# Rotary half-swaps and key doublings issued from ScalarE's queue instead of SyncE's, in a two-layer NSA/FoX decoder trunk

## The reference

```python
proj = x @ w_in
q, kc, vc, ks, vs, kw, vw, gl = jnp.split(proj, cuts, axis=-1)   # 16 query heads, 4 groups of keys and values
def apply_rope(x, cos, sin):
    x1, x2 = jnp.split(x, 2, axis=-1)
    return x * cos + jnp.concatenate([-x2, x1], axis=-1) * sin
q_rot = apply_rope(q, cos, sin)
k_slc = apply_rope(kv_heads(ks), cos, sin)
k_win = apply_rope(kv_heads(kw), cos, sin)
out = g0 * attend(q, k_cmp, v_cmp) + g1 * attend(q_rot, k_slc, v_slc) + g2 * attend(q_rot, k_win, v_win)
```

## Time and profile before

| | |
|---|---|
| median of 3 runs | 1443.62 us (1443.61 to 1446.38) |
| the profiled execution | 1443.62 us, span 1441.8 us |
| TensorE busy | 1366.0 us (95%) |
| VectorE, ScalarE, GpSimd busy | 691.6, 671.3, 624.6 us |
| DMAs issued by SyncE | 126.63 MB, 30.1% of 16 DMA engines' span |

### The profile page before, as it was taken

One profiled execution on the slowest core, in us unless ns is written; L12 is line 12 of the kernel. 1 busy time (PEld: TensorE's weight loads), 2 busy tenths in 40 slices (PEclk: granted clock), 3 DMA queues, 4 the chain that ended last, 5 costly groups with the idle time before them and its releaser, 6 DMA issues.

```text
span 1441.8 us, 20004 instructions
## 1 busy us (share of the span) xinstructions
PE 1366.0 (95%) x7050; PEld 1122.2 (78%) x7050; DVE 691.6 (48%) x1312; ACT 671.3 (47%) x1249; POOL 624.6 (43%) x402
## 2 busy tenths in 40 slices
PE   8979999977999999999999999998899999999997
PEld 5857777766788888888888787877788888888886
DVE  3346767767174344341008477788184443442006
ACT  4346767666234444443112576777334444443110
POOL 2356767663335444444434222221334444444441
PEclk9999999999999999999999999999999999999999
DMA  9432221210523332333232322121423333324221
GB/s 281 98 74 52 45 52 47 55 40 1 176 59 102 102 101 88 102 101 132 88 96 67 95 76 60 45 80 55 160 74 88 102 90 99 102 88 145 88 74 58
DMA packets 170237, 127.59 MB, mean 88 GB/s; under 512 B 24032, under 2 KB 155860, under 8 KB 170164
## 3 DMA queue, kind: packets, MB, share of 16 engines
q1 hardware_dynamic: 170164, 126.63, 30.1%
HBM read 116.98 MB, written 4.39 MB: 84 GB/s over the span
## 4 chain that ended last, share of the span: by engine, by line
PE 75%; DVE 14%; issue 3%; ACT 3%; POOL 2%; DMA 1%; SPq 1%; DVEq 0%; POOLq 0%; ACTq 0%
PE ps L924 14%; PE ps L926 14%; PE ps L925 14%; PE ps L1166 7%; PE ps L1165 7%; PE ps L1168 7%; PE ps L1086 2%; PE ps L1100 2%; DVE ptl L1439 2%; DVE xt L1579 2%; DVE negmax L1422 1%; DVE xt L1569 1%; DVE stats L1573 1%; DVE prob L1435 1%; PE ps L1053 1%
## 5 line engine op out<-in xcount | busy, mean ns | idle before, releaser
L463 POOL TENSOR_TENSOR wl<-raw,wh 128x1024 fp32r<-128x1024 f32 x180 | 437.1, 2432 | 675.5 <-ACT wh L582 675.3
L924 PE MATMUL ps<-xh,wh 128*128 128x512 f32 x968 | 392.0, 405 | 0.2 <-POOL wl L463 0.2
L926 PE MATMUL ps<-xh,wl 128*128 128x512 f32 x968 | 378.8, 391 | 0.0
L925 PE MATMUL ps<-xl,wh 128*128 128x512 f32 x968 | 377.8, 390 | 0.0
L582 ACT ACTIVATE wh<-raw 128x1024 fp32r<-128x1024 f32 x192 | 201.6, 1052 | 211.1 <-PE ps L1168 200.9
L926 PEld LDWEIGHTS ps<-xh,wl 128*128 128x128 f32 x968 | 182.1, 188 | 39.2
L924 PEld LDWEIGHTS ps<-xh,wh 128*128 128x128 f32 x968 | 184.1, 190 | 32.6 <-DVE xl L1363 0.4
L925 PEld LDWEIGHTS ps<-xl,wh 128*128 128x128 f32 x968 | 182.9, 189 | 32.1
L1600 DVE SCALAR_TENSOR_TENSOR work<-ps,conv,work 128x511 f32<-128x511 f32 x88 | 66.0, 750 | 221.2 <-ACT work L804 155.8
L1569 DVE SCALAR_TENSOR_TENSOR xt<-xt,ps 128x512 f32<-128x512 f32 x32 | 20.5, 682 | 256.5 <-PE ps L1168 256.3
L676 ACT ACTIVATE prob<-ps,negmax 128x128 f32<-128x128 f32 x192 | 101.1, 527 | 83.9 <-DVE negmax L1422 81.7
(11 more groups left out here) (192 smaller groups left out, 2074.6 us busy)
## 6 DMA issues: line engine op xcount, KB each, us to landing
raw<-in_ffn_w_up SPq DMA_DIRECT2D x88, 512.0 KB, 3.8
raw<-in_ffn_w_down SPq DMA_DIRECT2D x44, 512.0 KB, 3.5
raw<-in_fox_w_in SPq DMA_DIRECT2D x24, 512.0 KB, 4.1
raw<-in_nsa_w_in SPq DMA_DIRECT2D x12, 512.0 KB, 5.4
xt<-in_x SPq DMA_DIRECT2D x8, 512.0 KB, 6.5
raw<-in_nsa_w_in SPq DMA_DIRECT2D x16, 256.0 KB, 3.9
raw<-in_nsa_w_o SPq DMA_DIRECT2D x8, 512.0 KB, 3.9
raw<-in_fox_w_o SPq DMA_DIRECT2D x8, 512.0 KB, 3.5
```

The source lines that it names most:

```text
L463: nc.gpsimd.tensor_tensor(wl[:, slot, :, :], raw[:, slot, :, :], wh[:, slot, :, :].bitcast(F32), ALU.subtract).then_inc(s_wl, 1)
L924: nc.tensor.matmul(o, ah, bh, start=start, stop=False)
L925: nc.tensor.matmul(o, ah, bl, start=False, stop=False)
L926: return nc.tensor.matmul(o, al, bh, start=False, stop=stop)
```

## The change

The DMAs of `swap_halves` and `double_keys` are no longer issued in SyncE's program but in ScalarE's. Their number, shapes, sources, targets and the semaphores that they wait for and raise stay. In ScalarE's program the swap of item (0, 0) stands right behind its copy, as do those of (0, 2) and (0, 3); within the units a swap stands behind the `unit_hi` that follows the item's copy, at the eighth unit of an item; the doubling of group g+1 stands between the exp and the high copy of the sixth unit of its second item. SyncE's program keeps the loads, in the same order.

```diff
@@ SyncE
-            def swap_halves(n):
-                rn, k = n - (n + 2) // 4, n % 4
-                src = tmpf if k == 0 else qf[n // 4 % 2][:, k - 2, :]
...
-            for n in range(6):
-                load_item(n)
-                if n == 3:
+            for g in range(GROUPS):
+                c = 4 + 4 * g
+                for n, r0 in ((0, 0), (1, KV)):
+                    sp.wait_ge(s_wl, c + n - (R - 1))
+                    for b in range(2):
+                        sp.dma_start(raw[:, (c + n) % R, :, b * HD:(b + 1) * HD],
+                                     wsv[:, :, b, r0 + g * HD:r0 + (g + 1) * HD]).then_inc(s_raw[(c + n) % R], 16)
+                for n in range(2):
+                    load(c + 2 + n, (c + 2 + n) % R, cols(w_nsa, g * REP * HD + n * P))
+                if g == 0:
                     sp.wait_ge(s_vt, 6)
...
-            for n in range(6, NSA_ITEMS):
-                item_moves(n - 6)
-                load_item(n)
@@ def load_out
-                    if c0 == C_WO0 and k < 6:
-                        item_moves(NSA_ITEMS - 6 + k)
@@ ScalarE
+            def swap_halves(g, k):
+                n = 4 * g + k
+                rn = n - (n + 2) // 4
+                act.wait_ge(s_pf, n + 1)
+                if rn:
+                    act.wait_ge(s_r2, rn)
+                src = tmpf if k == 0 else qf[g % 2][:, k - 2, :]
+                q = HD // 2
+                for b in range(4):
+                    act.dma_start(swapped[b * q:(b + 1) * q, :], src[(b ^ 1) * q:((b ^ 1) + 1) * q, :]).then_inc(s_sr, 16)
...
+            def double_keys(g):
+                par = g % 2
+                act.wait_ge(s_pl, 4 * g + 1)
+                act.dma_start(ks[par][HD:P, :, :].bitcast(F32), ks[par][0:HD, :, :].bitcast(F32)).then_inc(s_sw[par], 16)
+                act.dma_start(kw[par][0:HD, :, :].bitcast(F32), kw[par][HD:P, :, :].bitcast(F32)).then_inc(s_sw[par], 16)
...
             item_copy(0, 0)
+            swap_halves(0, 0)
             hi(7, 7 % R)
...
             item_hi(0, 1)
+            double_keys(0)
             item_copy(0, 2)
+            swap_halves(0, 2)
             hi(9, 9 % R)
             item_hi(0, 2)
             cmp_exp(0)
             item_copy(0, 3)
+            swap_halves(0, 3)
...
+                    if w == 5 and turned and item[1] == 0:
+                        double_keys(item[0])
                     if g < GROUPS - 1 and w == 7:
                         item_copy(g + 1, v // 8)
                     unit_hi(u, w % 4)
+                    if g < GROUPS - 1 and w == 7 and v // 8 != 1:
+                        swap_halves(g + 1, v // 8)
```

## The result

The change made the kernel slower: 1455.56 us median of five runs, against 1443.62 us before; ratio 1.0079, 95% interval 1.0055 to 1.0101, so +11.4 us (7.9 to 14.6). The forecast was +4.2 us, with a range to 1455.0. The sign was right, but the measured loss is more than twice the forecast, and the median lies just above the range.

The account below looks back on a forecast made before the run. Bound by TensorE (75% of the chain that ended last; VectorE 14%). Prologue -1.8, group ends +4.2, mid-group swaps +1.5 and +0.3 sum to +4.2 us on 1443.62: 1447.8 us, range 1443.5 to 1455.

Parts of the forecast that it names:

- The landing of the mid-group swaps: Sine product behind mid-group swaps: about 0.4 us to spare, so nothing added if data still lands 2.0 us after issue.
- Rival 3: Swaps and weight loads collide: each of six mid-group swaps costs at most 0.6 us, +3.6, 1451.4 us; chance 0.10.
- the sum: All terms added, -1.8 + 4.2 + 1.5 + 0.3 = +4.2 us, giving 1447.8 us; chance 0.33.
- that rule of arbitration: Queues share 16 DMA engines packet by packet, so a swap is slowed, not held up; favours 1447.8 us over Rival 3.
- The hold in mid-group: Issues on ScalarE delay the exp in mid-group: 3 x 0.5 us at third items, 3 x 0.1 us at first items.
- rival 1: Issues run beside the high copy, group-end slip 0.92 instead of 1.40 us: +1.1 us, 1444.7 us; chance 0.18.
- The group ends: Four issues delay the exp, L736 and then TensorE by 1.40 us at three group ends: +4.2 us.
- rival 2: TensorE's clock falls at the first two group ends, 1.7 us lost each, up to +3.4: 1451.2 us; chance 0.20.
- The doublings: Three in the loop: 1.18 us of issues fit the exp's 1.22 us of idle time; count 0, up to 0.5 each.
- SyncE's queue without the moves: SyncE issues only weight loads; earlier loads gain nothing, counted 0.
- The prologue: The first swap, issued earlier, closes TensorE's 1.93 us hole before the value turn: -1.8 us.
- The bound of 0 for a swap that lands after 66: Lower limit of the prologue's gain: none if the first swap's data lands after 66 us.

Follow-up runs that it names:

- run 3: Kernel before with only the six mid-group swaps issued by ScalarE: 1448.03 us, ratio 1.0039.
- Run 6: Kernel before with the mid-group swaps on ScalarE and SyncE's weight load held back until the swap has landed: 1441.49 us, ratio 1.0002.
- Run 7: Kernel before, all moves on SyncE, but each weight load ahead of the swap in its queue: 1456.32 us, ratio 1.0106.
- run 4: Kernel before with only the three group-end swaps issued by ScalarE: 1449.75 us, ratio 1.0057.
- Run 5: As run 4, but two issues behind unit 31's high copy and two behind the copy of the compressed probabilities: 1442.01 us, ratio 0.9999.
- run 1: Kernel before with only group 0's four moves (three swaps, one doubling) issued by ScalarE: 1441.16 us, ratio 0.9997.
- run 8: Kernel before, all on SyncE, first swap ahead of the conv weights, later loads held back until the swap landed: 1440.80 us, ratio 0.9991.
- runs 1 to 4: run 1, run 3, run 4 and the kernel before with only the units' three doublings issued by ScalarE (1442.91 us, ratio 1.0000).
- run 9: The changed kernel, all 56 issues on ScalarE, with group-end issues in two pairs and later loads held until the swap landed: 1441.31 us, ratio 0.9991.

## Why the prediction was wrong, point by point

- **The landing of the mid-group swaps: the step that failed.** The prediction said that the sine product "adds nothing if the landing stays at 2.0 us". It did not stay: 3.7 us. The 2.0 us of the earlier trace rows was the landing of a swap that stood ahead of the load in one queue, so the row held only as long as the order did, and the change took the order away. Rival 3 named this and gave it 0.10, with a landing 1 us late and a price of at most 0.6 per swap. The wait was 1.25 to 1.75 us and the price 0.9 to 1.6 (0.5 at the place that was late before too), +5.6 us by run 3 where the sum had +1.8. Run 6 settles the cause: with the load held back the cost is gone, though ScalarE is held as before. Run 7 adds that late data costs as much and more with ScalarE free.
- **By that rule of arbitration.** The prediction quoted the Trainium skill (DMA: Bandwidth & Descriptors, Issuing engines are not separate DMA queues) as speaking for a swap only slowed and the 1447.8 of the sum. The transfers do share the engines as the page says, but a slowing from 2.0 to 3.7 us was the whole loss in mid-group. I had read "shared" as "harmless".
- **The hold in mid-group.** Booked at 3 x 0.5 + 3 x 0.1 = 1.8 us; measured 0 (run 6). The issues start beside the high copy, as rival 1 had it: at 165.38, while the high copy ran from 165.24 for 0.60 us. The Trainium skill (Perfetto Trace Analysis, DVE / Act Engine Instruction) says that the sequencer is ready for the next instruction once an activation is in the wait queue; the trace agrees, since the issues start 0.03 us behind the end of the copy that they wait for (164.76 + 0.59).
- **The group ends.** The chain was right: exp, L736, its low part, unit 31's low part, TensorE. The slip was 1.16 us, between rival 1's 0.92 and the sum's 1.40. But +8.2 us came out of it by run 4, not 4.2, so this term was mis-sized: it put nothing for the clock and took every issue at the median. Three slips are 3.5 us. By estimate the rest is the clock, 1.6 us at each of two group ends (rival 2, chance 0.20, with 1.7 us each), and about 1 us for the long issue. In the changed kernel's first profile, without a long issue and with one fall of the clock, it was 1.17 + 2.69 and up to 2.09. Run 5 shows that all of it hangs on the four issues in a row.
- **The doublings** cost 0, as said. **SyncE's queue without the moves** gains nothing for the loads, as said; what it lost was their place behind the swap, which the prediction's "I count 0" left out.
- **The prologue** was right in its mechanism and smaller: 1.30 us in the stretch (1.6 in run 1) instead of 1.8, since the first swap also landed late. In run 8, where it landed by 61.99, the stretch gained 2.0. The bound of 0 for a swap that lands after 66 was too pessimistic: it landed at 66.2.
- **How the chances were set.** Rivals 1, 2 and 3 were treated as alternatives with a forecast between them. All three came true together. They are different mechanisms at different places, so their prices should have been added with their chances. All three together give -1.8 + 2.8 + 0.1 + 3.4 + 3.6 = +8.1 us.

The parts add up: 5.6 + 8.2 - 0.4 + 0 = 13.4 us by the ratios of runs 1 to 4, each with an interval of 1.5 to 2.5 us to either side, within the interval of the change (7.9 to 14.6). With both cured no loss is left (run 9). Against the forecast's terms the mid-group swaps took 3.8 us more, the group ends 4.0 and the prologue 1.4, so the miss is not the landing's alone.

## What to carry to other kernels

A queue's order is a priority. When a small transfer that is waited for soon stands ahead of a large one that is not, moving either to another queue can set them off together, and the landing time read from the old trace (2.0 us here, then 3.7) no longer holds. When DMA issues go into a compute engine's program, count them in a row: at 0.61 us each beside the instruction ahead, the spare time before the next one (1.56 us from the high copy to the exp here) takes two and not four. And rivals at different places are to be added, not weighed against each other.

## What the runs showed of the hardware that was not expected

- ScalarE's DMA issues run beside its activation. In the changed kernel they started at 184.54, while the high copy ran from 184.48 for 0.60 us. What waits is the next activation in the list: the exp, 2.02 us until 187.09.
- A swap's 64 KB moves within the on-chip memory landed in 2.0 us (median) with the load held back or started behind the last issue, and in 3.6 to 3.9 us with 512 KB of weights started 0.7 to 1.2 us behind the first issue (as at 184.54 and 185.76).
- Behind nearly equal waits of TensorE (2.42 to 2.48 us) the granted clock fell in three of five cases and stayed up in two; what decides it was not found. Behind 3.42, 3.48 and 3.86 us it fell each time.
- One of the four issues at the first group end took 1.0 to 1.3 us longer than the median of 0.61 in three of four profiles. With two and two there, the longest took 0.77 (run 5) and 1.01 us (run 9). SyncE's issues of the same swap had it too (3.56 us for the four in run 6), so it is not tied to ScalarE's queue. Its cause stays open.
